# Two interleaved recurrences: small products, row loads, ScalarE's preparation and VectorE's pace in another order

## The reference

```python
for d, offset in enumerate((1, -1)):                      # two directions
    zd = z + mu[d] * (shift_seq(z, offset) - z)
    r, k, v, lw, la = split(zd)
    w_log = -softplus(-(w0[d] + tanh(lw) @ w2[d])) - 0.5
    decay = exp(-exp(w_log)); a = sigmoid(a0[d] + la @ a2[d])
    kk = k * k_k; kk = kk * rsqrt(max(sum(kk * kk), 1e-24))    # per head of 64
    k = k * (1 + (a - 1) * k_a)
def step(S, (r, w, k, v, a, b)):                          # a = -kk, b = kk * a
    sa = S @ a; S = S * w + outer(sa, b) + outer(v, k); y = S @ r
bonus = sum(r * k * r_k) * v
```

## Time and profile before

| what | before |
|---|---|
| median of 3 runs | 3390.03 us |
| the profiled execution, its own time | 3389.77 us |
| its span, first to last instruction | 3388.0 us |
| PE / PEld / DVE / ACT / POOL busy | 93 / 74 / 43 / 35 / 24% of the span |
| mean granted TensorE clock | 0.974 of full |
| DMA | 364.5 MB, mean 108 GB/s |
| the chain that ended last | PE 77%, DVE 6%, ACT 4%, DMA 2% |

### The profile page before, as it was taken

How to read it: one execution, slowest core, us unless ns; L and a number is a source line. 1 busy time by engine, 2 the same in 40 slices (tenths; PEclk the granted TensorE clock), 3 DMA queues, 4 the chain that set the end, 5 groups by cost and what they waited for, 6 DMA issues and landing times.

```text
span 3388.0 us, 77718 instructions
## 1 busy us (share of the span) xinstructions
PE 3137.5 (93%) x33614; PEld 2515.9 (74%) x33614; DVE 1465.6 (43%) x2262; ACT 1179.8 (35%) x2499; POOL 826.7 (24%) x518
## 2 busy tenths in 40 slices
PE   7999899899999998999999888989899989989998
PEld 5777677677777786888888666767677767768886
DVE  4455464644354662200044464656564446430033
ACT  4433333433333433311112353434343344342222
POOL 2211111111223132122223221111111233434453
PEclk9999999999999999999999989999999999999999
DMA  5424243334355352111111233414143343522222
GB/s 210 134 91 142 83 124 119 117 118 139 122 180 173 133 179 69 38 66 64 62 50 62 81 93 104 119 60 126 57 130 102 98 137 101 194 69 97 99 87 75
DMA packets 246709, 364.47 MB, mean 108 GB/s; under 512 B 154080, under 2 KB 155376, under 8 KB 245904
## 3 DMA queue, kind: packets, MB, share of 16 engines
q1 hardware_dynamic: 226976, 294.57, 27.2%
q10 hardware_dynamic: 14976, 35.66, 2.7%
q0 software_dynamic: 4464, 29.92, 2.5%
HBM read 290.88 MB, written 69.21 MB: 106 GB/s over the span
## 4 chain that ended last, share of the span: by engine, by line
PE 77%; DVE 6%; ACT 4%; issue 4%; DMA 2%; DVEq 2%; POOLq 1%; PEld 1%; SPq 1%; POOL 0%; PEldq 0%; ACTq 0%
PE banks L281 21%; PE banks L282 18%; PE banks L283 18%; PE banks L1673 2%; PE banks L1021 2%; PE banks L1684 1%; PE banks L1676 1%; PE banks L395 1%; PE banks L1637 1%; PE banks L1696 1%; PE banks L1733 1%; PE banks L2042 1%; POOLq L2413 1%; DVE arena L597 1%; PE banks L1049 1%
## 5 line engine op out<-in xcount | busy, mean ns | idle before, releaser
L283 PE MATMUL banks<-hx_rounded,slot_rounded 128*128 128x512 f32 (+1 forms) x1624 | 579.1, 357 | 0.0
L904 POOL TENSOR_TENSOR slot_rounded<-slot,branch_weights_high 128x512 fp32r<-128x512 f32 x188 | 245.6, 1328 | 1305.4 <-ACT branch_weights_high L899 1304.1
L281 PE MATMUL banks<-hx_high,weight_parts 128*128 128x512 f32 (+1 forms) x1512 | 538.1, 356 | 10.9 <-DVE hx_low L545 10.3
L281 PE MATMUL banks<-hx_rounded,branch_weights_high 128*128 128x512 f32 (+1 forms) x1280 | 501.1, 391 | 42.6 <-DVE arena L1362 7.4
L282 PE MATMUL banks<-hx_low,weight_parts 128*128 128x512 f32 (+1 forms) x1512 | 538.1, 356 | 0.0
L283 PE MATMUL banks<-hx_high,weight_parts 128*128 128x512 f32 (+1 forms) x1512 | 536.5, 355 | 0.0
L282 PE MATMUL banks<-resid_rounded,branch_weights_high 128*128 128x512 f32 (+1 forms) x1280 | 455.8, 356 | 0.0
L283 PEld LDWEIGHTS banks<-hx_rounded,slot_rounded 128*128 128x128 f32 x1624 | 314.2, 193 | 44.8
L281 PEld LDWEIGHTS banks<-hx_rounded,branch_weights_high 128*128 128x128 f32 x1280 | 247.8, 194 | 122.7 <-issue 74.5
L281 PEld LDWEIGHTS banks<-hx_high,weight_parts 128*128 128x128 f32 x1512 | 286.9, 190 | 54.9 <-issue 14.0
L283 PEld LDWEIGHTS banks<-hx_high,weight_parts 128*128 128x128 f32 x1512 | 286.3, 189 | 41.1
(11 more groups left out here) (261 smaller groups left out, 5824.1 us busy)
## 6 DMA issues: line engine op xcount, KB each, us to landing
slot<-in_w_mix SPq DMA_DIRECT2D x120, 512.0 KB, 3.9
slot<-in_w_ffn_in SPq DMA_DIRECT2D x88, 512.0 KB, 3.3
arena<-chunk_inputs SPq DMA_DIRECT2D x48, 640.0 KB, 4.4
arena<-in_w_ada SPq DMA_DIRECT2D x50, 512.0 KB, 5.0
slot<-in_w_ffn_out SPq DMA_DIRECT2D x44, 512.0 KB, 3.3
slot<-in_w_ada SPq DMA_DIRECT2D x40, 512.0 KB, 4.1
chunk_inputs<-arena SPq DMA_DIRECT2D x80, 256.0 KB, 3.8
arena<-side_projections POOLq DMA_DIRECT2D x16, 1152.0 KB, 6.4
```

The source lines that it names most:

```text
L281: first = nc.tensor.matmul(out, w_hi, x_hi, start=start, stop=False)
L283: return first, nc.tensor.matmul(out, w_lo, x_hi, start=False, stop=stop)
L904: last = nc.gpsimd.tensor_tensor(slots_r[g % 3][:, half], slots[g % 3][:, half], weights_high(g)[:, half], ALU.subtract)
```

## The change

No arithmetic changes; only order. In a body:

1. LEAD is 14. The body starts one chain visit earlier, so the blocks start at its visits 1, 9, 16, 24, 31 and 39.
2. PE's list has `decay_and_rate` after the segment-1 part of tiles 0 and 3 (before: ahead of tile 0, and after the one of tile 2), `key_norm` after that of tiles 1 and 4, `bonus_sum` after tile 2 and after the segment-1 part of tile 5. In layer 0 `bonus_sum` takes segment 1 first.
3. ACT's rounding comes last of its threads.
4. DVE's `pace` is 0.3, so three steps to a gap.
5. SP's list loads rows one tile earlier, apart from the tile's weights; the loads of tiles g0+4 and g0+5 stand behind `store(0, 0)` and `store(0, 1)`.

```diff
-        LEAD, LIVE = 15, 17
+        LEAD, LIVE = 14, 17
...
-            return [0, 1] if l == 0 and st == BODY else [1, 0]
+            return [0, 1] if l == 0 and st == BODY and what == "norm" else [1, 0]
...
                 elif st == BODY:
+                    yield from tile(0, 1)
                     yield from decay_and_rate(0)
-                    yield from tile(0, 1)
-                    yield from key_norm(0)
                     yield from tile(0, 0)
                     yield from tile(1, 1)
+                    yield from key_norm(0)
                     yield from tile(1, 0)
+                    yield from tile(2, 1)
+                    yield from tile(2, 0)
                     yield from bonus_sum(0)
-                    yield from tile(2, 1)
+                    yield from tile(3, 1)
                     yield from decay_and_rate(1)
-                    yield from tile(2, 0)
-                    yield from tile(3, 1)
-                    yield from key_norm(1)
                     yield from tile(3, 0)
                     yield from tile(4, 1)
+                    yield from key_norm(1)
+                    yield from tile(4, 0)
+                    yield from tile(5, 1)
                     yield from bonus_sum(1)
-                    yield from tile(4, 0)
-                    yield from tile(5)
+                    yield from tile(5, 0)
                     yield from gate_of_readout()
...
-            threads = [Thread(eviction()), Thread(rounding())] + ([Thread(preparation())] if st != TAIL else []) + ([Thread(readout())] if st != PRO else [])
+            threads = [Thread(eviction())] + ([Thread(preparation())] if st != TAIL else []) + ([Thread(readout())] if st != PRO else []) + [Thread(rounding())]
...
-                g, pace = -0.5, 0 if st == PRO else 0.5
+                g, pace = -0.5, 0 if st == PRO else 0.3
...
             elif st == BODY:
                 stage_load(hp, 3)
                 next_load(0)
+                next_rows(1)
                 store(0, 0)
+                next_tile(1)
+                stage_load(hp, 4)
                 store(1, 0)
-                next_load(1)
+                next_rows(2)
                 for o in (2, 3, 4):
                     store(o, 0)
-                stage_load(hp, 4)
                 store(0, 1)
-                next_load(2)
+                next_tile(2)
+                next_rows(3)
                 stage_load(hp, 5)
-                next_load(3)
+                next_tile(3)
+                next_rows(4)
                 store(1, 1)
-                next_load(4)
+                next_tile(4)
                 for o in (2, 3, 4):
                     store(o, 1)
                 stage_load(hq, 0)
```

More of the change, by code:

```diff
@@ L998, in program, with sum_order @@
         COST = [0.36, 0.68]
-        def sum_order(l, st):
-            return [0, 1] if l == 0 and st == BODY else [1, 0]
+        def sum_order(l, st, what):
+            return [0, 1] if l == 0 and st == BODY and what == "norm" else [1, 0]
         SHARE = [1.4 if r % LAG < 3 else 1.0 for r in range(PERIOD)]
@@ L1055, in key_norm @@
             def key_norm(d):
-                for i, s in enumerate(sum_order(l, st)):
+                for i, s in enumerate(sum_order(l, st, "norm")):
                     if i == 0:
@@ L1061, in bonus_sum @@
             def bonus_sum(d):
-                for i, s in enumerate([s for s in sum_order(l, st) if s in outs]):
+                for i, s in enumerate([s for s in sum_order(l, st, "bonus") if s in outs]):
                     if i == 0:
@@ L1505, in stage_load, with next_rows @@
                 sp.dma_start(STG.rearrange("p j o t -> p j (o t)"), ddx_dram[bass.ds(k * 2, 2)].rearrange("c p o t -> p c (o t)")).then_inc(staged.sem, 16)
-            def next_load(t):
+            def next_rows(t):
                 for c in rows_of(l, g0 + t):
@@ L1510, in next_load, with next_tile @@
                         rows_load(sp, c + 2)
+            def next_tile(t):
                 tile_load(sp, l, g0 + t + 3)
+            def next_load(t):
+                next_rows(t)
+                next_tile(t)
             g0 = FIRST_TILE[st, hp]
```

## The result

| what | before | after |
|---|---|---|
| median | 3390.55 us (4 runs, 3385.98 to 3392.58) | 3463.91 us (4 runs, 3458.99 to 3469.75) |
| ratio | | 1.0222, 95% interval 1.0203 to 1.0241 |
| span of the profiled execution | 3388.0 us | 3459.4 us |
| PE busy | 3137.5 us, 93% | 3135.6 us, 91% |
| mean granted clock | 0.974 | 0.968 |

The account below looks back on a forecast made before the run. PE, busy 93% of the span, was taken to bound the kernel, its idle time at most 110 us. From 3389.8 us, losses 54 + 39 + 12 less gains 42 gave +63: 3453 us, range 3395 to 3500.

Parts of the forecast that it names:

- main case: Both losses, A and B, outweigh the gains: 3453 us, own range 3425 to 3485, chance 0.58.
- R1: Rival: A without B, ScalarE's stand at the rounding short or covered: 3409 us, 3395 to 3425, chance 0.17.
- A: Next head pair's block 0: PE waits for the last array by way of DRAM, six waits, 54 us lost.
- B: ScalarE stands at the rounding for tile g0+5's late weights, PE behind its sigmoids: five waits, net 39 us lost.
- R3: Rival: PE's other work covers the last array's way, gains stand alone: 3348 us, faster, chance 0.10.
- R4: Rival: near zero, A at 40, B nearly nothing, gains 42: 3390 us, 3378 to 3400, chance 0.05.
- R2: Rival: both losses, clock down two or three times 3.4 us per wait, gains half: 3493 us, chance 0.10.
- gains: Shorter block-2, `decay_and_rate`, row and bonus-step waits, with the clock stretches behind them: 42 us gained together.
- clock, in the gains and behind the new waits: Half-clock stretches: eleven new waits at 1.7 us each, 19 less 7, cost 12; old stretches' removal counted in gains.
- my own lower bound: Lower bound of A: 40 us, if VectorE, with fewer block steps in visit 30 than in 25, comes 2 us earlier.
- (1): LEAD 14 starts block 2 one visit into the body, covering its late load: 12 us gained, bounds 5 to 15.
- (2): First `decay_and_rate` no longer at the body's start: six waits, 14 us, keep 1.3 each, 6.5 us gained.

Follow-up runs that it names:

- e1: Changed kernel with the weights of tile g0+5 loaded ahead of the stores of direction 0's last three arrays: 3404.1 us, 1.0045.
- e9: Kernel before, with VectorE's step for direction 1's last array held to gap 29, a lead of one visit: 3436.5 us, 1.0133.
- e4: Changed kernel with PE's list and the bonus order of before: 3378.3 us, 0.9973.
- e5: Kernel before with LEAD 14 alone: 3370.0 us, 0.9946.
- e10: Kernel before with LEAD 14 and the two rows of tile 2 asked for ahead of the store: 3348.3 us, 0.9878.
- e13: Changed kernel with the weights of tile g0+5 loaded ahead, and LEAD back at 15: 3452.6 us, 1.0194.
- e2: Changed kernel with a pace of 0.25 for VectorE's four steps behind direction 1's bonus step, last array due in gap 29: 3458.9 us, 1.0198.

## Why the prediction was right, and where its sizes were off

The forecast was 3453, range 3395 to 3500, with 0.85 on slower; measured 3463.9. Both mechanisms of the main case are there, where and as often as said, and e1, e9 and e4 show them one by one. R1 (A without B) and R3 (neither) fell with the rows above, and so did R4. Of R2 two parts came true: the stretches at the half clock behind the ten long waits are two to four times 3.4 us, and the gains were about half. It cost 30 us less than R2's price, since PE has little to do in those stretches. But the sum came near by errors that cancelled in part, and that is luck:

| term | predicted | measured |
|---|---|---|
| A, six waits | +54 | +39.0 |
| B, five waits, less the waits it replaces | +39 | +44.5 (56.1 less 11.5) |
| other waits, gains | -25 | about -10 |
| clock, in the gains and behind the new waits | -17 + 12 | about +0.5 |
| sum | +63 | +74; the medians differ by 73, the profiled executions by 71 |

**A.** The step that was wrong is the lead. "The array then ends 0.5 us after PE has arrived": it ended 1.9 us before, in each body of layer 0. I had scaled the lead from gap 25, in which VectorE has a young block's three steps to do; in gap 30 there is none such, which was my own lower bound. The path through DRAM was as read: 10.1, 10.3 and 9.7 us in layer 0, where the kernel before has 10.2, 9.8 and 10.3. In bodies 1 and 2 of layer 1 the array ended 2.2 and 1.6 us before PE arrived, not 0.3, and body 2's path was 7.9 us. The 4.3 of body 0 was 0.5: a lead of 8.1 us over a path of 8.6.

**B.** 11.8 against 10.7 us in layer 0, 10.4 against 9.4 in layer 1. The weights' load took 4.65 us (487.47 to 492.12), not the median of 3.9, with the stores beside it. Everything else of that sum held within 0.4 us.

**Gains.** The row waits went, as said. Of (1), 3.26 us went to nothing in layer 0, but layer 1 kept 2.55 of 3.19. Of (2), the first `decay_and_rate` of layer 0 still waits for the eviction ahead of it (0.84) and for its last sigmoids (1.07), 1.9 where I took 1.3. And new small waits came that I had not seen. In body 0 of layer 1 PE waits 3.76 us at the bonus sum and starts it 0.1 us after VectorE has made the product that it sums. At the readout's gate PE waits 2.49 us in body 0 and 3.19 in body 1, and that is loss B once more, small: the load of a further tile stands behind `store(1, 1)`, ScalarE stands for it, and the copy that frees the gate's bank (L1242) is queued behind.

```profile
2402.56 1.06 ACT L899 ACTIVATE branch_weights_high<-slot 128x1024 fp32r<-128x1024 f32 x1 [3.77 <-DMA slot<-in_w_mix]
...
2405.73 0.77 PE L281 MATMUL banks<-hx_rounded,branch_weights_high 128*128 128x512 f32 x1 [3.19 <-ACT arena L1242]
```

I had asked "what waits behind this load" of two loads of the list and not of all.

**The clock.** These terms held. I had charged each of eleven new waits 1.7 us, 19 in all, and counted 24 for old stretches that go (17 in the gains and 7 behind the second `decay_and_rate`). Counted in each layer from its first block to its last, PE's busy time at the half clock is 61 us before and 62 after. Of the 62, 42 lie in the stretches of the ten long waits, worth 21; the other stretches have 20 left of 61, worth 20. These are two of the ten, behind B and behind A in layer 0:

```profile
279.00:292.70 13.70, 4.50 (x33) 4.30 (x34) 0.60 (x1) 3.92 (x5) 2.50 (x2) 0.50 0.48 154
343.90:350.70 6.80, 2.77 (x11) 2.57 (x12) 0.00 (x0) 1.61 (x8) 0.00 (x0) 0.50 0.89 316
```

The first is 13.7 us long, but PE is busy for 4.5 of it: the clock falls while PE stands, and a long wait eats most of its own stretch. In the earlier trace rows PE is busy for 6.1 of 6.8 and 8.7 of 10.2 us, since the waits there are short. So what a stretch costs is half of PE's busy time in it, and not half of its length, as I took it in the upper bound of 40 and in what I expected of e1. Ten waits of 6 to 12 us cost no more clock than the dozen of 2 to 3 us had. The same count explains the gains that e5 and e10 had beyond their waits (36 and 10 us).

**The DMA rule.** By the fit in the Trainium skill (DMA: Bandwidth & Descriptors, Anatomy of one DMA), read as one store and one load, loss A would have been an estimated 34 and not 54 us; measured 39. That it comes nearer is chance: in the trace the stores and the load took 10.3 us, not 6.1, and what made A smaller was the lead.

## What to carry to other kernels

Where engines follow fixed lists, write down for each hand-over the gap in which it is made and the gap in which it is wanted, and move producer and consumer together: both losses here are lines of that table in which the order had turned (17 before 18) or the lead had shrunk to less than the path through DRAM. Ask of each wait what stands behind it on its engine; an entry of the load queue that is moved behind a late store delays an engine that has nothing to do with that store. Try the parts alone: of five edits two were worth 39 us, and the others cost 115.

## What the runs showed that I had not expected

- A long wait costs less clock than several short ones: a stretch of 13.7 us at 1.2 GHz behind a wait of 12.2 us held 4.5 us of PE's work, one of 10.2 us behind waits of 3.3 and 1.4 held 8.7.
- A start one chain visit earlier gave 18 us, though PE's idle time fell by 8 us only; the rest is time at the half clock, which is no longer there where two pauses had been neighbours.
- Taking away the last visit of lead (e13) cost only 1.3 to 1.7 us more at each place in layer 0, where a visit is 4.05: the lead shrank by 3.5 us, but the path through DRAM was some 2 us shorter.
- Six stores of up to 256 KB issued in a row took from 539.50 to about 549.4 us to land, and an end of the last array 1.3 us earlier changed that by 0.3 (e2).
- ScalarE stood 8.43 us for a load and PE lost nothing by it, in another place 3.77 us and PE lost 3.19: the queue behind the stand decides.
